# Attention in a streaming encoder step: the weighted values of unit n-1 ahead of the turned probabilities and denominators of unit n

## The reference

```python
z = rms_norm(x, norm_g) @ w_in                    # u | q | k | v
s = einsum(q, k) * HEAD_DIM ** -0.5 - slope * |distance|, masked to the band
m = maximum(max(s), sink)
p = exp(s - m)
denom = sum(p) + exp(sink - m)
o = einsum(p / denom, v)
h = x + concatenate([pool_mix(u), o]) @ w_out
y = h + (silu(hn @ w_gate) * (hn @ w_up)) @ w_down      # hn = rms_norm(h)
```

## Time and profile before

| | us |
|---|---|
| median of 3 runs | 2290.54 |
| lowest run | 2288.74 |
| highest run | 3587.15 |
| profiled execution | 2290.56 |
| its span, first to last instruction | 2288.8 |
| mean granted TensorE clock | 0.998 of full speed |
| TensorE busy | 2223.7 (97%) |
| VectorE, ScalarE, GpSimd busy | 956.7, 759.3, 642.5 |

### The profile page before, as it was taken

The page is one execution under the profiler, slowest core; times in us unless marked ns, Lnnn a source line. Parts: engine busy times, 40 slices in busy tenths (PEclk is TensorE's granted clock), DMA queues, the critical chain, the costliest instruction groups (busy, mean ns, idle before and its releaser), DMA issues.

```text
span 2288.8 us, 32450 instructions
## 1 busy us (share of the span) xinstructions
PE 2223.7 (97%) x12667; PEld 1997.5 (87%) x12667; DVE 956.7 (42%) x1685; ACT 759.3 (33%) x1601; POOL 642.5 (28%) x296
## 2 busy tenths in 40 slices
PE   7999999999999999999999999999999899999999
PEld 6876799999999989767999999999887689999998
DVE  3558713322222255586222332222566753434244
ACT  4575422121121235764312112111357442222221
POOL 2410332223223214112332323223141224333331
PEclk9999999999999999999999999999999999999999
DMA  4110231212112133002321212211331223223221
GB/s 135 47 38 1 93 111 56 73 55 73 55 55 75 37 122 109 19 19 92 93 70 59 73 55 66 62 56 56 102 107 38 82 74 102 83 75 90 73 74 42
DMA packets 194378, 159.97 MB, mean 70 GB/s; under 512 B 7005, under 2 KB 176906, under 8 KB 194282
## 3 DMA queue, kind: packets, MB, share of 16 engines
q1 hardware_dynamic: 191326, 149.58, 21.3%
q10 hardware_dynamic: 2956, 9.08, 1.0%
HBM read 149.66 MB, written 9.07 MB: 69 GB/s over the span
## 4 chain that ended last, share of the span: by engine, by line
PE 83%; DVE 8%; ACT 5%; issue 2%; POOL 1%; DMA 1%; SPq 0%; DVEq 0%; ACTq 0%; POOLq 0%
PE ps L597 26%; PE ps L599 26%; PE ps L598 26%; DVE s_sb L1479 2%; ACT s_sb L1107 2%; DVE negmax L1484 1%; DVE xn L1343 1%; PE ps L694 1%; PE ps L732 1%; POOL w_lo L501 1%; PE ps L710 1%; DVE h L1355 1%; DVE kt_sb L1402 1%; PE ps L611 1%; DVE xt_lo L1331 1%
## 5 line engine op out<-in xcount | busy, mean ns | idle before, releaser
L501 POOL TENSOR_TENSOR w_lo<-raw,w_hi 128x1024 fp32r<-128x1024 f32 x249 | 596.9, 2417 | 1497.9 <-ACT w_hi L980 863.1
L597 PE MATMUL ps<-xt_hi,w_hi 128*128 128x384 f32 (+1 forms) x2640 | 859.4, 326 | 2.9 <-issue 1.8
L599 PE MATMUL ps<-xt_hi,w_lo 128*128 128x384 f32 (+1 forms) x2640 | 852.8, 323 | 0.0
L598 PE MATMUL ps<-xt_lo,w_hi 128*128 128x384 f32 (+1 forms) x2640 | 852.5, 323 | 0.0
L597 PEld LDWEIGHTS ps<-xt_hi,w_hi 128*128 128x128 f32 x2640 | 497.7, 189 | 10.7 <-issue 4.9
L598 PEld LDWEIGHTS ps<-xt_lo,w_hi 128*128 128x128 f32 x2640 | 497.8, 189 | 2.6 <-issue 0.3
L599 PEld LDWEIGHTS ps<-xt_hi,w_lo 128*128 128x128 f32 x2640 | 497.4, 188 | 0.0
L1355 DVE TENSOR_TENSOR h<-ps,h 128x512 f32<-128x512 f32 (+1 forms) x510 | 348.7, 689 | 239.0 <-PE ps L599 237.4
L1567 DVE TENSOR_TENSOR aa<-ps,sg 128x384 f32<-128x384 f32 (+1 forms) x132 | 69.2, 524 | 823.7 <-PE ps L599 821.9
L1202 ACT ACTIVATE sg<-ps 128x384 f32<-128x384 f32 (+1 forms) x132 | 61.3, 464 | 663.1 <-PE ps L599 663.0
L597 PE MATMUL ps<-w_hi,act_hi 128*128 128x512 f32 x704 | 279.6, 397 | 0.0
(11 more groups left out here) (131 smaller groups left out, 1760.2 us busy)
## 6 DMA issues: line engine op xcount, KB each, us to landing
raw<-in_w_gate SPq DMA_DIRECT2D x66, 512.0 KB, 3.8
raw<-in_w_up SPq DMA_DIRECT2D x66, 512.0 KB, 4.0
raw<-in_w_down SPq DMA_DIRECT2D x66, 512.0 KB, 3.2
raw<-in_w_in SPq DMA_DIRECT2D x33, 512.0 KB, 4.0
raw<-in_w_out SPq DMA_DIRECT2D x24, 512.0 KB, 4.1
h<-in_x_prompt SPq DMA_DIRECT2D x16, 512.0 KB, 7.5
out<-h ACTq DMA_DIRECT2D x16, 512.0 KB, 2.7
xload<-in_x_prompt SPq DMA_DIRECT2D x10, 512.0 KB, 3.5
```

Of the source, the lines that this page charges most:

```text
L501: nc.gpsimd.tensor_tensor(lo, raw, hi.bitcast(F32), ALU.subtract).then_inc(done, 1)
L597: nc.tensor.matmul(out, w_hi, m_hi, start=first, stop=False)
L598: nc.tensor.matmul(out, w_hi, m_lo, start=False, stop=False)
L599: return nc.tensor.matmul(out, w_lo, m_hi, start=False, stop=last)
```

## The change

In each of the three loops `attend` one call changes places with its neighbour, so that the work of unit n-1 comes ahead of that of unit n: the weighted values ahead of the turned probabilities on TensorE, the denominator copy ahead of the probability copy on ScalarE, the output ahead of the denominators on VectorE. All helpers, their waits and their buffers stay as they are.

```diff
@@ -822,10 +822,10 @@
                     if n == s.mix_at:
                         pool_map(s, 0)
-                    prob_transposes(s, n)
                     t = n - s.out_at
                     if n >= 1:
                         weighted_values(s, n - 1)
+                    prob_transposes(s, n)
                     if n >= s.mix_at:
                         late_sums(s, n)
@@ -1167,9 +1167,9 @@
                         late_rstd(s, n)
-                    prob_copy(s, n)
                     if n >= 1:
                         denominator_copy(s, n - 1)
+                    prob_copy(s, n)
                     t = n - s.out_at
@@ -1541,10 +1541,10 @@
                     if n == s.mix_at:
                         pool_low(s, 0)
-                    denominators(s, n)
                     t = n - s.out_at
                     if n >= 1:
                         outputs(s, n - 1)
+                    denominators(s, n)
                     if not s.dense_first(n):
                         late_normed(s, n)
```

## The result

The change makes the kernel slower: 2299.02 us (median of 6 runs, 2298.33 to 2301.83) against 2289.55 (median of the 6 runs of before beside it, one of which, at 3587.15 us, stands far from the rest), a ratio of 1.0045 with a 95% interval of 1.0032 to 1.0059. That is 9.5 us more. Forecast were 2286.1 and a range up to 2292.0, so the sign of the difference was wrong and the time lies outside the range; only that it would stay within 2% came true. The profiled execution has a span of 2297.0 us (before: 2288.8).

The account below looks back on a forecast made before the run. TensorE, busy 97%, was taken as the bound, with 21.9 us of attention gaps to win and a ScalarE-VectorE loop in the slab stage. Parts 0 and 1 at -1.65 each and part 2 at -1.15 gave -4.45: 2286.1 us, range 2284 to 2288.5 (2282.5 to 2292 with rivals).

Parts of the forecast that it names:

- Collisions: VectorE's L1497 against GpSimd's L551, both moved later: some dissolve, others arise, nought +-0.5 us per part.
- The slack of the denominators: At n=10, rden(9) ready about 0.2 us before the weighted values; last unit, denominators ready at 226.55, products at 227.05.
- The loop: ScalarE and VectorE, slab stage: net -0.22 us per turn; three turns in parts 0 and 1, six in part 2.
- The term of -0.91: Slab stage: ScalarE's probability copy leaves the chain as the denominator copy goes first, 0.91 us less per turn.
- The +0.69: Slab stage: VectorE's denominators come behind the output and ahead of the next scores, 0.69 us more per turn.
- TensorE's turnaround: Scores directly behind transposes: 0.2 us each, bounds 0.1 and 0.26, in 7+7+6 iterations; mostly covered by waits.
- Out stage: L710 stalls of parts 0 and 1 covered: -0.6 us at n=10, -0.6 at n=16 after a new L1355 wait.
- the shift of w_lo (L1516): Out stage, n=14 of parts 0 and 1: VectorE's w_lo shifts earlier by the same 0.6 us as TensorE.
- The last unit: End of each part: the 1.01 us idle before the last values is exchanged for another stall, -0.15 us a part.
- A: Rival, exchanged stalls: denominators behind the output load VectorE's chain, only the 0.15s stay, 2290.1 us; chance 0.24 including no change.
- B: Rival, slower: TensorE's transposes-to-scores turnaround is on the path, 0.26 us each, 2295.8 or 2292.9 us; chance 0.15.
- C: Rival: slab loop gives the full 0.91 as VectorE hides the denominators, some -4 us more, 2282; chance 0.09.

Follow-up runs that it names:

- e4: Changed kernel, with GpSimd's low-part weight blocks waiting for the same iteration's denominators in every iteration with a block: 2284.90 us, ratio 0.9978.
- e7: Changed kernel, with 18 useless TensorE products filling the stall ahead of weighted_values(mix_at-1): 2296.70 us, ratio 1.0030.
- e1: Changed kernel with VectorE's order put back (denominators ahead of output), TensorE and ScalarE swaps kept: 2275.97 us, ratio 0.9939.
- e9: Kernel before with TensorE's and ScalarE's swaps, plus GpSimd's blocks waiting for the denominators each time: 2276.61 us, ratio 0.9946.
- e8: Kernel before, no swaps, with GpSimd's blocks waiting for the denominators each time, as control: 2291.63 us, ratio 1.0008.
- T alone: Kernel before with TensorE's swap only, weighted values ahead of the probability transposes: 2299.23 us, ratio 1.0035.
- A alone: Kernel before with ScalarE's swap only, denominator copy ahead of the probability copy: 2281.41 us, ratio 0.9958.
- e2: Kernel before with VectorE's swap only, output ahead of the denominators: 2312.93 us, ratio 1.0097.

## Why the prediction was wrong

**Collisions: the step that failed.** The prediction put them at nought, +-0.5 us a part, in its sum. The runs show 14.1 us for those with L501 (after less e4), the clock behind the stalls included. The mechanism was in the rows: the earlier trace rows show L1497 tripled by a GpSimd instruction, and the Trainium skill (SBUF — State Buffer, Who interferes with whom) has the two exclude each other for a whole instruction. The trace of after agrees, with 2.18 us for a copy of 0.29 under a block of 2.3. The failure was to price it by L551, the 0.74 us instruction of the row, and by a symmetry ("some dissolve, others arise"). The longest GpSimd instruction near the moved work was L501, 2.4 us, two in a row; the places it takes in each part were in the trace, and the output's start in VectorE's iteration mix_at - 1 (164.32, inside the pair 161.81 to 166.51) was where the denominators would land. It was also taken for granted that only the copy is held; the four-column addition L1495 is held as well and lasts up to 1.79 us. The trace of before had a sign of it: its longest L1495 took 431 ns, the median 155.

**The slack of the denominators.** Moved from idle time to the last moment before L722, a delay of theirs becomes TensorE's at once. The prediction worked out that slack for n=10 (0.2 us) and for the last unit, but not at n=2 and mix_at - 1. The waits for these came to 1.72 and 2.76 in part 0, 1.30 and 2.33 in part 1, and 4.60 for mix_at - 1 in part 2. Of the last, 2.07 us are a second miss, without any collision (e4).

**Stalls have a price beyond their length.** The clock was not in the sum, neither what it takes behind the new stalls nor what it gives back where the waits at n=5 shrink; e7 returned 2.3 us.

**The loop: right by the turn.** Forecast -0.22 a turn; L1479 in part 0 of after starts at 125.09, 131.67 and 139.09, in before at 124.42, 131.30 and 139.01: turns of 6.58 and 7.42 against 6.88 and 7.71, -0.3 each. The term of -0.91 is right: e1's turn, which has no other, is 0.92 shorter than that of before. The +0.69 is 0.62 in the same turn (6.58 less 5.96). Summed over the slab stages it is 3.5 us and not 8.3 (e9), so not all of the 12 turns pass it on.

**TensorE's turnaround: size right.** From L710 to L694 in after are 1.03 us (120.59 to 121.62) where eight transposes took 0.87: +0.16, forecast 0.2 between 0.1 and 0.26. Whether it stayed hidden was not measured apart; e1, which has the same pairs, is 14.2 us under before, so it can't be the loss.

**Out stage: right.** The stalls at n=10 and n=16 are gone, and the new wait on L1355 at n=17 is there, 0.50 and 0.45 us (forecast 0.6). What was too small is the shift of w_lo (L1516): TensorE waits 1.0 us longer for it in sum (2.3 to 3.3 us):

```profile
221.88 0.47 PE L597 MATMUL ps<-w_hi,xt_hi 128*128 128x512 f32 x1 [0.50 <-DVE h L1355]
...
227.84 0.41 PE L722 MATMUL ps<-ident,xload 128*128 128x128 f32 x2 [0.69 <-DVE xload L1497]
```

**The last unit: right in parts 0 and 1.** The second of these rows of after's timeline is the exchanged stall, 0.69 (part 1: 0.69) for 1.01 before. In part 2 it is 1.07, so nothing is gained there.

**The sum without the failed term.** -4.45 forecast, -6.7 measured (e4 less e8, each known to some 2 us): the same within the noise. But e4 holds the 2.07 us that the forecast did not have, and e4's lower level of the clock lasts 3 us against 14 in e8, worth at most 5 us. So the agreement is of the sum, and not of every term.

**The rivals.** None of them was it. A had the VectorE chain loaded by the denominators, but let only gains vanish. B had the sign, but looked for the loss at the turnaround, which e1 has as well without losing. C named the gain of the full 0.91; that comes true only in a kernel that leaves the denominators where they were (e1, -14 us), and there it was more than its 4 us, as there is no collision in the slab stage that counts, TensorE's waits for squares fall to 0.4 us, and the lower level of the clock lasts 3 us instead of 10, worth at most 3.5 us.

**The better kernel.** e1 beats both: 2276 us, 0.6% under before. It is the change without its third part.

## What to carry over

When work moves within an engine's queue, look up what the other engines do at its new time, and price a possible conflict by the longest instruction that lies there, not by the one seen in a collision so far. Work done in idle time ahead of need should stay there: its slack is what absorbs such conflicts. A reordering over several engines is to be tried engine by engine, since one part can outweigh the others and parts can need each other (T alone +9.3, A alone -8.5, both -14.2).

## What the runs showed of the hardware

- An addition of 128x4 float32 from SBUF, 0.15 us, lasted 1.79 us, and 2.20 in e2, under a 128x1024 operation of GpSimd. The size of VectorE's instruction didn't protect it. Instructions of VectorE that read PSUM (L1507 0.42, L1479 1.40 for four) kept their times under the same block.
- Two GpSimd blocks in a row held two VectorE instructions one after the other (L1495 0.81, L1497 2.18), with 0.24 us between them in which VectorE ran.
- The three stalls of TensorE at mix_at (2.76, 2.33 and 4.60 us) each brought a stretch at the lower granted clock (0.66 to 0.70 in the mean of 4 to 7 us), while the mean over the span still read 0.995. In part 0 the clock fell 1.4 us after the stall had ended, in part 2 during it. A wait is not always followed by one: the same wait for squares in part 1, 2.02 us in before and 2.00 in e8, was in before and was not in e8. The slower transposes in the timeline (seven in 1.62 us, against eight in 1.1) show it sooner than the mean does.
